# Weighing the values of a dilated attention: three split-precision products over the whole array, or plain fp32 with each head on its own half of the columns

## The chip, the cores and the metric

One core of a Trainium2 chip runs the whole program. The metric is the device time of one execution in microseconds (us). Engines are named as the profile names them: PE is TensorE (PEld its weight loads), DVE VectorE, ACT ScalarE, POOL GpSimd, SP SyncE.

## The reference, cut to what matters

One inference step of a two-layer decoder over a prompt of 1024 tokens and 8 sampled tokens. The change touches only the first mixer, and there the prompt. It projects the input to queries, keys and values for three dilation branches (window 128 and dilation 1, 512 and 4, 2048 and 16) and 16 heads of 64 features; each query reads at most 129 keys, which lie in its own block of 128 keys of its residue class and in the one before:

```python
s = jnp.einsum('nbqhd,nbphd->nhbqp', qb, kk).astype(jnp.float32) * SCALE
...
probs, lse = masked_softmax_lse(s, mask)
o = jnp.einsum('nhbqp,nbphd->nbqhd', probs, vv)     # the product that the change touches
...
y = merge_by_denominator(outs, lses).astype(x.dtype).reshape(B, S, N_HEADS_A * HEAD_DIM) @ w_o
```

After the mixer come a layer norm, a gated feed-forward part, a second mixer and a second feed-forward part. All inputs and outputs are fp32.

## The kernel before

**Split precision.** Most products are made of three: a value `a` is kept as `a_hi` (a cast to fp32r) and `a_lo` (the rest, `a - a_hi`, as fp32r), and `product` (lines 99 to 103) adds `w_hi*x_hi`, `w_hi*x_lo` and `w_lo*x_hi` in one bank. ACT writes the high parts, DVE or POOL the low ones. A few products take plain fp32 operands: those of the sampled tokens with their caches (`key_four`, line 1024; `value_four`, line 1062; a small one in the second mixer, line 2476). These, and their like for the sampled tokens of the second mixer, are the only ones that put several results on different columns of the array at a time, by `tile_position` or by the partitions that they write: four groups of 16 or 32 columns in the first two, two groups of 64 in the third.

**Order of the first mixer.** The work is cut into 24 items `i`, each a pair of heads `q` (8 pairs) and a dilation branch `g` (3). An item has 4 steps `s`, so there are 96 steps `u`; each attends two tiles of 128 queries (`j` = 0, 1), for both heads `h` of the pair. The order of each engine's queue is written out by hand in `body(u, i, s)`. On PE a step is: `scores(u)`, `weigh_values(u - 2)`, `transpose_probs(u - 1)`, in the first two steps of an item `transpose_v`, sometimes one or two small products that spread merge factors (`spread_factors`, line 911), and then two or three `chunk`s of the projection of the next item (line 101 to 103, 24 matmuls each of 352 or 328 columns). In the last four steps there is no next item, and `key_four` stands in the place of the chunks. After the steps come `value_four` and the merging of the last pair.

**The product of the change.** A query tile reads one or two key blocks `b`: two, except where its class has no block before it. That makes 35 blocks for each head pair over the three branches. For each block `weigh_values` runs one `product`: stationary operand `v_hi[:, kt, :]` or `v_lo`, 128 keys by 128 features (both heads side by side), moving operand 256 columns of turned probabilities `pt_hi` or `pt_lo` (128 queries of head 0, then 128 of head 1). The result is `pv_bank`, 128 feature rows by 2 x 2 x 128 columns, in which only the feature rows of head `h` with the query columns of head `h` are wanted. So half of the bank is never read. `evacuate_o` on ACT copies the wanted parts, 64 rows by 256 columns for each head.

**Around it.** ACT's `high_probs` and DVE's `low_probs` make `pt_hi` and `pt_lo` from the turned probabilities in `pt_bank`, `high_v` and `low_v` do it for the values in `x_bank`. In DVE's queue `low_probs(u - 1)` stands behind `mask_scores(u)` and ahead of `merge_tile`, whose product `a_fbm` (line 734) must be done before PE may run the next `spread_factors`.

Of the kernel before, what the change touches and what calls it, by code (L numbers as in the profile page):

```python
# [24 lines left out]
P = 128  # L25
# [30 lines left out]
def f32(ap):  # L56
    return ap.bitcast(F32)
# [105 lines left out]
def mixer_a(nc, x_hi, x_lo, dram, s_roll):  # L163
    ctx = ExitStack()
    sems = []
    with ctx:
# [9 lines left out]
        raw = sb("raw", [P, 2, KT, P])  # L176
        v_hi = sb("v_hi", [P, QT, P], F32R)
        v_lo = sb("v_lo", [P, QT, P], F32R)
        vt = sb("vt", [P, T])
# [8 lines left out]
        sp = sb("sp", [P, 2, 2, 2, 2 * P])  # L188
        pt_hi = sb("pt_hi", [P, 2, 4 * P], F32R)
        pt_lo = sb("pt_lo", [P, 2, 4 * P], F32R)  # L190
        o = sb("o", [P, 2, NG, T])
# [15 lines left out]
        with ExitStack() as lent:  # L207
# [20 lines left out]
        kq_out = [sem("kq_out0"), sem("kq_out1")]  # L228
        s_vout, s_vtr, s_vhi, s_vlo = (sem(x) for x in ("vout", "vtr", "vhi", "vlo"))
        s_scores, s_masked, s_probs, s_ptr, s_pthi, s_ptlo, s_pv, s_oev = (  # L230
            sem(x) for x in ("scores", "masked", "probs", "ptr", "pthi", "ptlo", "pv", "oev"))
        s_sttr, s_stcp, s_stout, s_srin, s_dve, s_dd, s_mw, s_f, s_fb, s_fbm, s_fbr, s_oout = (
# [210 lines left out]
        def _(act):  # L443
# [37 lines left out]
            def evacuate_o(u):  # L481


                i, s = divmod(u, SUPER)
                q, g = pair_group(i)
                need(act, s_pv, 2 * u + 2)
                if g == 0 and s == 0:
                    need(act, s_oout, 16 * (q - 1))
                for h in range(2):
                    rows = slice(HD * h, HD * h + HD)  # L490
                    src = pv_bank[rows, :].rearrange("p (i x q) -> p i x q", i=2, x=2)[:, :, h, :]
                    last = act.copy(pair_tokens(o[rows, q % 2, g, 0:SEQ], g, s), pair_shape(src, g))
                last.then_inc(s_oev, 1)

            def high_probs(u):
                need(act, s_pv, 2 * u)
                for j in range(2):
                    c0 = 2 * first_key(u, j)
                    need(act, s_ptr, 2 * u + j + 1)
                    act.copy(pt_hi[:, j, c0:], pt_bank[j][:, c0:]).then_inc(s_pthi, 1)  # L500

            def high_v(u, i, s):
                need(act, s_vtr, 2 * i + s + 1)
                need(act, s_pv, 2 * (u - 1))
                act.copy(v_hi[:, 4 * s:4 * s + 4, :].rearrange("p a b -> p (a b)"), x_bank[:, :]).then_inc(s_vhi, 1)

# [33 lines left out]
            def body(u, i, s):  # L540
                q, g = pair_group(i)
                if s in SPLIT_AT and 3 * (i + 1) + SPLIT_AT[s] < NB:
                    split_w(3 * (i + 1) + SPLIT_AT[s])
                if attends(u):
                    exponentials(u)
                if u == NU + 1:
                    copy_last_stats(0)
                if attends(u - 2):
                    evacuate_o(u - 2)
                if attends(u - 1):  # L550
                    high_probs(u - 1)
                if attends(u) and s < 2:
                    high_v(u, i, s)
# [100 lines left out]
        def _(dve):  # L654
# [99 lines left out]

            def low_probs(u):
                for j in range(2):
                    c0 = 2 * first_key(u, j)
                    need(dve, s_pthi, 2 * u + j + 1)
                    dve.tensor_tensor(pt_lo[:, j, c0:], pt_bank[j][:, c0:], f32(pt_hi[:, j, c0:]),
                                      ALU.subtract).then_inc(s_ptlo, 1)  # L760

            def low_v(i, s):
                need(dve, s_vhi, 2 * i + s + 1)
                dve.tensor_tensor(v_lo[:, 4 * s:4 * s + 4, :].rearrange("p a b -> p (a b)"), x_bank[:, :],
                                  f32(v_hi[:, 4 * s:4 * s + 4, :].rearrange("p a b -> p (a b)")),
                                  ALU.subtract).then_inc(s_vlo, 1)

            def turn(i1, r):
# [10 lines left out]
            def body(u, i, s):  # L779
# [17 lines left out]
                if attends(u) and s < 2:  # L797
                    low_v(i, s)
                if attends(u) and q > 0 and g == 1 and s < 2:
# [76 lines left out]
        def _(pe):  # L876
            def stats_transpose(q):
                need(pe, s_probs, 4 * NG * SUPER * q)
                need(pe, s_vlo, 2 * min(NG * q + 1, NI))
                need(pe, s_fbm, 8 * (q - 1))  # L880
                pe.transpose(x_bank[0:96, 0:P], st[:, (q - 1) % 2, :], ident[:, :]).then_inc(s_sttr, 1)

            def spread_stats(w):
# [5 lines left out]
                else:  # L889
                    pe.wait_ge(s_ptlo, 2 * NU)  # L890
                to = last_bank[w]
# [12 lines left out]
            def spread_factors(q, j):  # L904
# [3 lines left out]
                if j in (0, 4):  # L908
                    need(pe, s_vlo, 2 * min(NG * q + 2 + j // 4, NI))
                need(pe, s_fbm, 8 * (q - 1) + j)  # L910
# [20 lines left out]
            def weigh_values(u):  # L931
                i, s = divmod(u, SUPER)
                need(pe, s_oev, u)
                if s in (0, 2):
                    need(pe, s_vlo, 2 * i + 1 + s // 2)
                for j in range(2):
                    need(pe, s_ptlo, 2 * u + j + 1)
                    b0 = first_key(u, j) // P
                    for b in range(b0, 2):
                        kt = 2 * s + j - 1 + b  # L940
                        cols = slice(b * 2 * P, (b + 1) * 2 * P)
                        last = product(pe, pv_bank[:, 2 * P * j:2 * P * (j + 1)], v_hi[:, kt, :], v_lo[:, kt, :],
                                       pt_hi[:, j, cols], pt_lo[:, j, cols], b == b0, b == 1)
                    last.then_inc(s_pv, 1)

            def transpose_probs(u):
                for j in range(2):
                    need(pe, s_probs, 4 * u + 2 * j + 2)
                    need(pe, s_ptlo, 2 * (u - 1) + j + 1)
                    for b in range(first_key(u, j) // P, 2):  # L950
# [5 lines left out]
            def transpose_v(i, s):  # L956
                need(pe, s_evac, 9 * (i + 1))
                need(pe, s_vlo, 2 * i + s)
                q, g = pair_group(i)
# [85 lines left out]
            def value_four(n):  # L1045
# [9 lines left out]
                if n == NG:  # L1055
                    pe.wait_ge(s_ptlo, 2 * NU)
                    pe.wait_ge(s_lcp, 2)
# [1624 lines left out]
```

## Time and profile before

| what | value |
|---|---|
| median of 3 runs | 3226.95 us (3219.56 to 3236.51) |
| the profiled execution: from its first to its last instruction | 3217.9 us |
| first mixer, steps and end | up to about 1200 us of it |
| PE, PEld busy | 97%, 94% |
| DVE, ACT, POOL busy | 54%, 49%, 53% |

The profiled execution gives no time of its own beside its span; 3217.9 us is 1.7 us under the fastest of the three runs and 9.1 us under their median. In a row of a timeline a group of equal instructions is one row: its start, the time from its first start to its last end, and xN for their number. A matmul's own duration runs on into the next ones (they are pipelined), so what one costs is the distance from start to start. A plain fp32 matmul is two records, with two weight loads.

### The profile page before, as it was taken

How to read it: one execution, taken by the hardware profiler on the slowest of the kernel's cores; microseconds unless marked ns; L12 is line 12 of the kernel's file. 1: busy time of each engine (PE TensorE's matmuls, PEld its weight loads, DVE VectorE, ACT ScalarE, POOL GpSimd, SP SyncE). 2: the span in 40 equal slices, each digit the busy share in tenths (PEclk: the TensorE clock that was granted, in tenths of full speed). 3: DMA queues.
4: the chain of work that ended last, by engine and by line, in shares of the span. 5: the costliest groups of instructions: out<-in, count | busy, mean ns of one | idle time of the engine just before them, and what ended most of it. 6: DMA issues, size and time to landing. Idle time of an engine off the chain costs nothing. (4 is left out here: it accounts for less than half of the span.)

```text
span 3217.9 us, 55825 instructions
## 1 busy us (share of the span) xinstructions
PE 3111.2 (97%) x21245; PEld 3033.5 (94%) x21245; DVE 1729.2 (54%) x3649; ACT 1590.6 (49%) x3331; POOL 1701.3 (53%) x1421
## 2 busy tenths in 40 slices
PE   8999999999999979999999999999899999999997
PEld 7999999999999959999999999988799999999997
DVE  4445555454555546665363365389866653533653
ACT  4555555555555524454353354367745543533542
POOL 5555555555555604665465466454246654554653
PEclk9999999999999989999999999999999999999998
DMA  5766676677667385444444444321153444444442
GB/s 210 251 246 209 229 266 218 224 247 248 235 225 273 101 302 183 131 133 132 139 134 138 138 141 146 111 62 41 41 197 128 137 130 139 152 138 136 163 152 95
DMA packets 134218, 540.86 MB, mean 168 GB/s; under 512 B 24336, under 2 KB 48544, under 8 KB 131120
## 3 DMA queue, kind: packets, MB, share of 16 engines
q1 hardware_dynamic: 133440, 536.51, 49.3%
q8 instruction: 170, 2.79, 0.4%
q14 instruction: 96, 0.79, 0.1%
q0 software_dynamic: 224, 0.26, 0.1%
q10 hardware_dynamic: 288, 0.52, 0.0%
HBM read 497.55 MB, written 216.85 MB: 222 GB/s over the span
## 5 line engine op out<-in xcount | busy, mean ns | idle before, releaser
L1369 ACT CAST w_hi<-raw 128x1024 fp32r<-128x1024 f32 (+1 forms) x459 | 471.3, 1027 | 841.7 <-PE bank L103 795.6
L101 PE MATMUL bank<-x_hi,w_hi 128*128 128x352 f32 (+1 forms) x2208 | 711.9, 322 | 5.2 <-POOL w_lo L1487 3.9
L1568 DVE TENSOR_TENSOR w_lo<-raw,w_hi 128x1024 fp32r<-128x1024 f32 (+1 forms) x229 | 320.7, 1401 | 735.9 <-ACT w_hi L1369 735.8
L102 PE MATMUL bank<-x_lo,w_hi 128*128 128x352 f32 (+1 forms) x2208 | 705.9, 320 | 0.0
L103 PE MATMUL bank<-x_hi,w_lo 128*128 128x352 f32 (+1 forms) x2208 | 702.5, 318 | 0.0
L1487 POOL TENSOR_TENSOR w_lo<-raw,w_hi 128x1024 fp32r<-128x1024 f32 (+1 forms) x230 | 546.8, 2377 | 276.0 <-ACT w_hi L1369 276.0
L101 PE MATMUL a_gemm<-x_hi,a_w_hi 128*128 128x352 f32 (+1 forms) x1728 | 560.5, 324 | 11.1 <-DVE x_lo L659 11.1
L102 PE MATMUL a_gemm<-x_lo,a_w_hi 128*128 128x352 f32 (+1 forms) x1728 | 553.3, 320 | 0.0
L103 PE MATMUL a_gemm<-x_hi,a_w_lo 128*128 128x352 f32 (+1 forms) x1728 | 551.4, 319 | 0.0
L101 PE MATMUL bank<-t_h_hi,w_hi 128*128 128x352 f32 (+1 forms) x1440 | 465.0, 323 | 6.8 <-POOL t_h_lo L1507 5.6
L103 PE MATMUL bank<-t_h_hi,w_lo 128*128 128x352 f32 (+1 forms) x1440 | 461.9, 321 | 0.0
L102 PE MATMUL bank<-t_h_lo,w_hi 128*128 128x352 f32 (+1 forms) x1440 | 460.2, 320 | 0.0
L101 PEld LDWEIGHTS bank<-x_hi,w_hi 128*128 128x128 f32 x2208 | 414.8, 188 | 8.3 <-POOL w_lo L1487 5.0
L102 PEld LDWEIGHTS bank<-x_lo,w_hi 128*128 128x128 f32 x2208 | 415.3, 188 | 1.6
L103 PEld LDWEIGHTS bank<-x_hi,w_lo 128*128 128x128 f32 x2208 | 415.0, 188 | 0.0
L101 PEld LDWEIGHTS a_gemm<-x_hi,a_w_hi 128*128 128x128 f32 x1728 | 325.7, 188 | 13.5 <-issue 9.2
L102 PEld LDWEIGHTS a_gemm<-x_lo,a_w_hi 128*128 128x128 f32 x1728 | 326.0, 189 | 0.0
L103 PEld LDWEIGHTS a_gemm<-x_hi,a_w_lo 128*128 128x128 f32 x1728 | 325.3, 188 | 0.0
L1507 POOL TENSOR_TENSOR t_h_lo<-t_acc,t_h_hi 128x352 fp32r<-128x352 f32 (+1 forms) x132 | 129.0, 977 | 332.9 <-ACT t_h_hi L1391 332.9
L101 PEld LDWEIGHTS bank<-t_h_hi,w_hi 128*128 128x128 f32 x1440 | 273.5, 190 | 9.2 <-issue 7.8
L750 DVE CUSTOM_DVE_ANT_0 a_sp<-a_scores,a_mask 128x128 f32<-128x128 f32 (+1 forms) x384 | 112.1, 347 | 304.4 <-PE a_scores L103 303.8
L102 PEld LDWEIGHTS bank<-t_h_lo,w_hi 128*128 128x128 f32 x1440 | 272.9, 190 | 0.9 <-issue 0.5
(303 smaller groups left out, 5693.1 us busy)
## 6 DMA issues: line engine op xcount, KB each, us to landing
raw<-w_up SPq DMA_DIRECT2D x264, 512.0 KB, 3.6
roll<-cache SPq DMA_DIRECT2D x128, 1023.5 KB
raw<-w_down SPq DMA_DIRECT2D x96, 512.0 KB, 3.5
a_raw<-w_a SPq DMA_DIRECT2D x72, 512.0 KB, 3.6
roll<-cache SPq DMA_DIRECT2D x16, 2044.0 KB
raw<-w_o SPq DMA_DIRECT2D x48, 512.0 KB, 3.5
raw<-w_down SPq DMA_DIRECT2D x48, 384.0 KB, 3.2
vT<-a_vt SPq DMA_DIRECT2D x24, 516.0 KB, 5.9
```

What stands on the lines that cost most here:

```text
L101: pe.matmul(out, w_hi, x_hi, start=first, stop=False)
L102: pe.matmul(out, w_hi, x_lo, start=False, stop=False)
L103: return pe.matmul(out, w_lo, x_hi, start=False, stop=last)
L750: dve.tensor_tensor_reduce(out=sp[:, u % 2, j, h, w0:], in0=s_bank[h][:, 2 * P * j + w0:2 * P * (j + 1)], in1=mk, scale=1.0, scalar=3.0e38 ...
L1369: act.copy(w_hi[:, b % RING, cols], raw[:, b % RING, cols]).then_inc(s_whi, 1)
L1487: pool.tensor_tensor(w_lo[:, b % RING, cols], raw[:, b % RING, cols], f32(w_hi[:, b % RING, cols]), ALU.subtract).then_inc(s_wlo[0], 1)
L1507: pool.tensor_tensor(h_lo[:, m, 0:n], acc[:, unit(c, m) % 3, 0:n], f32(h_hi[:, m, 0:n]), ALU.subtract).then_inc(s_hlo, 1)
L1568: dve.tensor_tensor(w_lo[:, b % RING, cols], raw[:, b % RING, cols], f32(w_hi[:, b % RING, cols]), ALU.subtract).then_inc(s_wlo[1], 1)
```

## The change

The values `v` and the turned probabilities `pt` are kept as one fp32 tile each; `v_lo`, `pt_lo` and the two DVE functions that made them are gone, and ACT's cast becomes a copy of the same size. `weigh_values` runs, for each block and head, one plain fp32 matmul: stationary `v[:, kt, rows]`, 128 keys by the 64 features of that head, moving 128 columns of that head's probabilities, written to partitions `rows` of the bank by `tile_position=(0, 64*h)`. Only wanted results are made, and `evacuate_o` copies them in one instruction of 128 rows. What waited for DVE's semaphores (`s_ptlo`, `s_vlo`) waits for ACT's (`s_pt`, `s_vev`).

```diff
-            def high_probs(u):
+                src = pv_bank[:, 0:2 * P].rearrange("p (i q) -> p i q", i=2)
+                act.copy(pair_tokens(o[:, q % 2, g, 0:SEQ], g, s), pair_shape(src, g)).then_inc(s_oev, 1)
+
+            def turned_probs(u):
                 need(act, s_pv, 2 * u)
                 for j in range(2):
                     c0 = 2 * first_key(u, j)
                     need(act, s_ptr, 2 * u + j + 1)
-                    act.copy(pt_hi[:, j, c0:], pt_bank[j][:, c0:]).then_inc(s_pthi, 1)
+                    act.copy(pt[:, j, c0:], pt_bank[j][:, c0:]).then_inc(s_pt, 1)
...
-            def low_probs(u):
-                for j in range(2):
-                    c0 = 2 * first_key(u, j)
-                    need(dve, s_pthi, 2 * u + j + 1)
-                    dve.tensor_tensor(pt_lo[:, j, c0:], pt_bank[j][:, c0:], f32(pt_hi[:, j, c0:]),
-                                      ALU.subtract).then_inc(s_ptlo, 1)
...
-                if attends(u - 1):
-                    low_probs(u - 1)
...
                 for j in range(2):
-                    need(pe, s_ptlo, 2 * u + j + 1)
+                    need(pe, s_pt, 2 * u + j + 1)
                     b0 = first_key(u, j) // P
                     for b in range(b0, 2):
                         kt = 2 * s + j - 1 + b
-                        cols = slice(b * 2 * P, (b + 1) * 2 * P)
-                        last = product(pe, pv_bank[:, 2 * P * j:2 * P * (j + 1)], v_hi[:, kt, :], v_lo[:, kt, :],
-                                       pt_hi[:, j, cols], pt_lo[:, j, cols], b == b0, b == 1)
+                        for h in range(2):
+                            c, rows = (2 * b + h) * P, slice(HD * h, HD * h + HD)
+                            last = pe.matmul(pv_bank[rows, P * j:P * (j + 1)], v[:, kt, rows], pt[:, j, c:c + P],
+                                             start=(b == b0), stop=(b == 1), tile_position=(0, HD * h))
                     last.then_inc(s_pv, 1)
```

PE's queue in a step of the third branch with two blocks and no `transpose_v` (`a_scores` is the scores bank, `a_pv` the product of the change, `a_probsT` the turning of the probabilities, `a_gemm` the projection), before:

```order
L102 MATMUL a_scores<-a_kq_lo,a_kq_hi 128x128
L103 MATMUL a_scores<-a_kq_hi,a_kq_lo 128x128
L101 MATMUL a_pv<-a_pt_hi,a_v_hi 128x256
L102 MATMUL a_pv<-a_pt_lo,a_v_hi 128x256
L103 MATMUL a_pv<-a_pt_hi,a_v_lo 128x256
L101 MATMUL a_pv<-a_pt_hi,a_v_hi 128x256
L102 MATMUL a_pv<-a_pt_lo,a_v_hi 128x256
L103 MATMUL a_pv<-a_pt_hi,a_v_lo 128x256
L953 MATMUL a_probsT<-a_ident,a_sp 128x128 x4
L101 MATMUL a_gemm<-x_hi,a_w_hi 128x328
```

and now:

```order
L102 MATMUL a_scores<-a_kq_lo,a_kq_hi 128x128
L103 MATMUL a_scores<-a_kq_hi,a_kq_lo 128x128
L921 MATMUL a_pv<-a_pt,a_v 64x128 x4
L932 MATMUL a_probsT<-a_ident,a_sp 128x128 x4
L101 MATMUL a_gemm<-x_hi,a_w_hi 128x328
```

The place in the queue is the same; six matmuls of 256 columns have become four of 128 columns, which are eight records, since they are plain fp32.

DVE's queue in the last but one step of the last item (u = 94; `a_sp,a_st` are the masked scores, `a_fbm` and `a_o` the two halves of `merge_tile`), before:

```order
L750 ISA a_st 128x1
L759 TENSOR_TENSOR a_pt_lo<-a_probsT,a_pt_hi 128x256 x2
L734 TENSOR_TENSOR a_fbm<-a_vT_factors,a_o 128x384
L737 TENSOR_REDUCE a_o<-a_fbm 128x128
L734 TENSOR_TENSOR a_fbm<-a_vT_factors,a_o 128x384
L737 TENSOR_REDUCE a_o<-a_fbm 128x128
L750 ISA a_sp,a_st<-a_scores,a_mask 128x128
```

and now:

```order
L745 ISA a_st 128x1
L729 TENSOR_TENSOR a_fbm<-a_vT_factors,a_o 128x384
L732 TENSOR_REDUCE a_o<-a_fbm 128x128
L729 TENSOR_TENSOR a_fbm<-a_vT_factors,a_o 128x384
L732 TENSOR_REDUCE a_o<-a_fbm 128x128
L745 ISA a_sp,a_st<-a_scores,a_mask 128x128
```

The two `a_pt_lo` instructions, which waited for ACT, no longer stand between the masking and the merge.

## Rows read from the trace of the kernel before

**Rows 1.** The page, its head and busy times.

```profile
span 3217.9 us, 55825 instructions
...
PE 3111.2 (97%) x21245; PEld 3033.5 (94%) x21245; DVE 1729.2 (54%) x3649; ACT 1590.6 (49%) x3331; POOL 1701.3 (53%) x1421
```

**Rows 2.** Windows: stretch, its length, busy us (instructions) by engine, PEclk, DMA share, GB/s.

```profile
100.00:1110.00 1010.00, 1008.25 (x7258) 979.07 (x7256) 520.93 (x1522) 573.57 (x1556) 553.06 (x459) 1.00 0.65 227
...
1200.00:3217.90 2017.90, 1950.63 (x12642) 1924.86 (x12642) 1123.28 (x1914) 943.77 (x1591) 1077.88 (x889) 0.99 0.40 130
```

**Rows 3.** Waits of PE, 100 to 1110 us: total us, times, longest.

```profile
PE a_vT_factors L911 <- DVE a_fbm L734: 1.8, 2, 1.6
```

**Rows 4.** All instructions that touch a_pv (two lines): duration ns min/median/max.

```profile
L101 PE MATMUL a_pv<-a_pt_hi,a_v_hi x280: 277/280/580, 76.1 to 1156.2; 128*128 128x256 f32 x140
...
L492 ACT COPY a_o<-a_pv x192: 345/590/642, 79.2 to 1157.4; 64x256 f32<-64x256 f32 x192
```

**Rows 5.** Timeline of PE, one step: start us, us.

```profile
607.12 0.29 PE L103 MATMUL a_scores<-a_kq_hi,a_kq_lo 64*128 64x256 f32 x2
607.34 0.39 PE L101 MATMUL a_pv<-a_pt_hi,a_v_hi 128*128 128x256 f32 x1
607.56 0.28 PE L102 MATMUL a_pv<-a_pt_lo,a_v_hi 128*128 128x256 f32 x1
...
608.03 0.28 PE L103 MATMUL a_pv<-a_pt_hi,a_v_lo 128*128 128x256 f32 x1
608.15 0.60 PE L953 MATMUL a_probsT<-a_ident,a_sp 128*128 128x128 f32 x4
```

**Rows 6.** Timeline of PE, first and last rounds of one key_four (plain fp32, four column groups).

```profile
1120.58 0.28 PE L1024 MATMUL a_gemm<-a_raw,a_cos 128*16 128x128 f32 x1
1120.58 0.30 PE L1024 MATMUL a_gemm<-a_units_kv,a_cos 128*16 128x128 f32 x3
...
1120.70 0.29 PE L1024 MATMUL a_gemm<-a_units_kv,a_cos 128*16 128x128 f32 x3
...
1122.23 0.29 PE L1024 MATMUL a_gemm<-a_units_kv,a_cos 128*16 128x128 f32 x3
```

**Rows 7.** Timeline of PEld at the same place: the loads of the third round.

```profile
1120.70 0.11 PEld L1024 LDWEIGHTS a_gemm<-a_units_kv,a_cos 128*16 128x16 f32 x3
```

**Rows 8.** Timeline, then the source line: plain fp32 on two 64-column halves, in the second mixer.

```profile
2327.18 0.31 PEld L2476 LDWEIGHTS bank<-b_d_own_x,b_d_om 128*64 128x64 f32 x8
2327.18 0.43 PE L2476 MATMUL bank<-b_d_own_x,b_d_om 128*64 128x32 f32 x8
...
L2476 PEld LDWEIGHTS bank<-b_d_own_x,b_d_om x8: 133/137/138, 2327.2 to 2327.4; 128*64 128x64 f32 x8
```

**Rows 9.** Groups of ACT and DVE, 100 to 1110 us: busy us, mean ns, idle before.

```profile
L538 ACT COPY a_vt<-a_gemm 128x352 f32<-128x352 f32 x43 | 19.5, 453 | 9.5 <-PE a_gemm L103 9.4
...
L759 DVE TENSOR_TENSOR a_pt_lo<-a_probsT,a_pt_hi 128x512 fp32r<-128x512 f32 x81 | 53.9, 688 | 38.1 <-ACT a_pt_hi L500 35.7
```

**Rows 10.** Waits of PE, 1110 to 1200 us, two of them.

```profile
PE a_vT_factors L911 <- DVE a_fbm L734: 6.0, 6, 1.8
...
PE a_scores L1062 <- DMA a_units_kv<-cache: 3.2, 1, 3.2
```

**Rows 11.** Timeline of DVE, then of PE, in step u = 94.

```profile
1136.67 0.08 DVE L750 DVE_READ_ACCUMULATOR2_ANT a_st<- 128x1 f32 x1
1139.31 0.76 DVE L759 TENSOR_TENSOR a_pt_lo<-a_probsT,a_pt_hi 128x256 fp32r<-128x256 f32 x2 [2.56 <-ACT a_pt_hi L500]
1139.98 0.55 DVE L734 TENSOR_TENSOR a_fbm<-a_vT_factors,a_o 128x384 f32<-128x384 f32 x1
...
1140.58 0.44 PE L911 MATMUL a_vT_factors<-a_f_both,a_sel 128*128 128x384 f32 x1 [1.47 <-DVE a_fbm L734]
```

**Rows 12.** Windows of ten us in the mixer's end; columns as in rows 2.

```profile
1140.00:1150.00 10.00, 6.27 (x107) 5.49 (x107) 7.01 (x21) 5.02 (x16) 0.00 (x0) 1.00 0.81 304
1150.00:1160.00 10.00, 9.10 (x176) 7.88 (x176) 3.96 (x13) 3.25 (x8) 0.00 (x0) 0.83 1.02 407
```

More of the change, by code:

```diff
@@ L176, in mixer_a @@
         raw = sb("raw", [P, 2, KT, P])
-        v_hi = sb("v_hi", [P, QT, P], F32R)
-        v_lo = sb("v_lo", [P, QT, P], F32R)
+        v = sb("v", [P, QT, P])
         vt = sb("vt", [P, T])
@@ L188, in mixer_a @@
         sp = sb("sp", [P, 2, 2, 2, 2 * P])
-        pt_hi = sb("pt_hi", [P, 2, 4 * P], F32R)
-        pt_lo = sb("pt_lo", [P, 2, 4 * P], F32R)
+        pt = sb("pt", [P, 2, 4 * P])
         o = sb("o", [P, 2, NG, T])
@@ L228, in mixer_a @@
         kq_out = [sem("kq_out0"), sem("kq_out1")]
-        s_vout, s_vtr, s_vhi, s_vlo = (sem(x) for x in ("vout", "vtr", "vhi", "vlo"))
-        s_scores, s_masked, s_probs, s_ptr, s_pthi, s_ptlo, s_pv, s_oev = (
-            sem(x) for x in ("scores", "masked", "probs", "ptr", "pthi", "ptlo", "pv", "oev"))
+        s_vout, s_vtr, s_vev = (sem(x) for x in ("vout", "vtr", "vev"))
+        s_scores, s_masked, s_probs, s_ptr, s_pt, s_pv, s_oev = (
+            sem(x) for x in ("scores", "masked", "probs", "ptr", "pt", "pv", "oev"))
         s_sttr, s_stcp, s_stout, s_srin, s_dve, s_dd, s_mw, s_f, s_fb, s_fbm, s_fbr, s_oout = (
@@ L488, in evacuate_o @@
                     need(act, s_oout, 16 * (q - 1))
[L489 to L493, printed above, removed]
-            def high_probs(u):
+                src = pv_bank[:, 0:2 * P].rearrange("p (i q) -> p i q", i=2)
+                act.copy(pair_tokens(o[:, q % 2, g, 0:SEQ], g, s), pair_shape(src, g)).then_inc(s_oev, 1)
+            def turned_probs(u):
                 need(act, s_pv, 2 * u)
@@ L499, in high_probs, with evacuate_v @@
                     need(act, s_ptr, 2 * u + j + 1)
-                    act.copy(pt_hi[:, j, c0:], pt_bank[j][:, c0:]).then_inc(s_pthi, 1)
-            def high_v(u, i, s):
+                    act.copy(pt[:, j, c0:], pt_bank[j][:, c0:]).then_inc(s_pt, 1)
+            def evacuate_v(u, i, s):
                 need(act, s_vtr, 2 * i + s + 1)
                 need(act, s_pv, 2 * (u - 1))
-                act.copy(v_hi[:, 4 * s:4 * s + 4, :].rearrange("p a b -> p (a b)"), x_bank[:, :]).then_inc(s_vhi, 1)
+                act.copy(v[:, 4 * s:4 * s + 4, :].rearrange("p a b -> p (a b)"), x_bank[:, :]).then_inc(s_vev, 1)
             def high_turned(i1, r):
@@ L550, in body @@
                 if attends(u - 1):
-                    high_probs(u - 1)
+                    turned_probs(u - 1)
                 if attends(u) and s < 2:
-                    high_v(u, i, s)
+                    evacuate_v(u, i, s)
                 if stats_due(i, s):
@@ L753, in mask_scores @@
                                                  accum_out=st[:, q % 2, c:c + 1]).then_inc(s_masked, 1)
-            def low_probs(u):
-                for j in range(2):
-                    c0 = 2 * first_key(u, j)
-                    need(dve, s_pthi, 2 * u + j + 1)
-                    dve.tensor_tensor(pt_lo[:, j, c0:], pt_bank[j][:, c0:], f32(pt_hi[:, j, c0:]),
-                                      ALU.subtract).then_inc(s_ptlo, 1)
[L762 to L766, printed above, removed]
             def turn(i1, r):
@@ L792, in body @@
                     replicate_stats(0)
-                if attends(u - 1):
-                    low_probs(u - 1)
                 if u == NU:
                     replicate_stats(1)
-                if attends(u) and s < 2:
-                    low_v(i, s)
                 if attends(u) and q > 0 and g == 1 and s < 2:
@@ L878, in stats_transpose @@
                 need(pe, s_probs, 4 * NG * SUPER * q)
-                need(pe, s_vlo, 2 * min(NG * q + 1, NI))
+                need(pe, s_vev, 2 * min(NG * q + 1, NI))
                 need(pe, s_fbm, 8 * (q - 1))
@@ L889, in spread_stats @@
                 else:
-                    pe.wait_ge(s_ptlo, 2 * NU)
+                    pe.wait_ge(s_pt, 2 * NU)
                 to = last_bank[w]
@@ L908, in spread_factors @@
                 if j in (0, 4):
-                    need(pe, s_vlo, 2 * min(NG * q + 2 + j // 4, NI))
+                    need(pe, s_vev, 2 * min(NG * q + 2 + j // 4, NI))
                 need(pe, s_fbm, 8 * (q - 1) + j)
@@ L934, in weigh_values @@
                 if s in (0, 2):
-                    need(pe, s_vlo, 2 * i + 1 + s // 2)
+                    need(pe, s_vev, 2 * i + 1 + s // 2)
                 for j in range(2):
-                    need(pe, s_ptlo, 2 * u + j + 1)
+                    need(pe, s_pt, 2 * u + j + 1)
                     b0 = first_key(u, j) // P
@@ L948, in transpose_probs @@
                     need(pe, s_probs, 4 * u + 2 * j + 2)
-                    need(pe, s_ptlo, 2 * (u - 1) + j + 1)
+                    need(pe, s_pt, 2 * (u - 1) + j + 1)
                     for b in range(first_key(u, j) // P, 2):
@@ L957, in transpose_v @@
                 need(pe, s_evac, 9 * (i + 1))
-                need(pe, s_vlo, 2 * i + s)
+                need(pe, s_vev, 2 * i + s)
                 q, g = pair_group(i)
@@ L1055, in value_four @@
                 if n == NG:
-                    pe.wait_ge(s_ptlo, 2 * NU)
+                    pe.wait_ge(s_pt, 2 * NU)
                     pe.wait_ge(s_lcp, 2)
```

## The prediction

> **What bounds the kernel now.** I read the page first, for who is busy: PE 97% of a span of 3217.9 us, the others about half [rows 1]. A share is an average over stages, so windows come next: from 100 to 1110 us, where the first mixer's steps run, PE is busy for 1008.25 of 1010 us, while DVE, ACT and POOL have 521 to 574 us of work [rows 2]. Busy is not yet bound, since matmuls overlap, so the third view is PE's waits in that stretch: 1.8 us in all [rows 3]. There PE's queue alone sets the pace, at full clock (1.00, that is 2.4 GHz), and what it is spared there shortens the program. From 1200 us on nothing is changed. From 1110 to 1200 us, the mixer's end, PE does wait: 6.0 us for DVE's merge, 3.2 us in one piece for a transfer [rows 10]; there the sum must be made otherwise.
>
> So the question is what the product of the change costs on PE, from start to start, with what stands before and behind it. A timeline of one step shows it [rows 5]. Between neighbours of the old product the distance is 0.118 us (607.56 to 608.03 is four distances, 0.47). From the last scores matmul (607.12) to the second of the product (607.56) there are 0.44 us where two steps at pace would be 0.24: changing from the scores' form (64 rows of the array, two at once) to the full array costs 0.20 us. It comes in two equal parts: the array runs empty (607.34 is 0.22 behind 607.12, 0.10 more than pace), and then the first weight load has nothing to hide behind (0.22 to the next start, 0.10 more than pace). From the product to the turning of the probabilities (608.03 to 608.15) there is no such cost; both use the full array.
>
> **The change on PE.** There are 280 blocks [rows 4] in 96 steps (192 copies by ACT, two a step [rows 4]).
> - Removed: three matmuls a block, 3 x 0.118 = 0.354 us.
> - Added: two plain fp32 matmuls a block, each two records. What a record of 128 moving columns costs is shown by the sampled tokens' keys, plain fp32 too: rounds start at 1120.58 and 1122.23, first and last of 16, so 1.65 / 15 = 0.110 us a round [rows 6], and a round is four records on four column groups (one and three in the rows). So a record takes 0.110 us of its own group, and groups run beside each other. For two halves a block then takes two rounds: 0.220 us. Saved: 0.134 x 280 = 37.5 us.
> - Are 64-column weight loads hidden? Each record has one. In the second mixer eight of them, on two halves, take 0.31 us in all and 0.137 each [rows 8]: (0.31 - 0.137) / 3 = 0.058 us from pair to pair if they go in pairs, and one behind the other they would be 0.025 apart, which is less than half of what a full 128-column load shows (0.10, above). So they go in pairs, 0.058 us each, and that fits under a pass of 0.110. That loads run under a pass on the same group is seen in the keys: the loads of the third round start at 1120.70, with the second round of matmuls and not behind it [rows 6, 7]. The record of 64 columns with 128 moving ones is in no row; it lies between the keys (16 columns) and the full array (128 columns, whose loads of 0.10 are hidden under 0.118), and I take it as hidden.
> - Moved: the forms now change twice in a step. Scores to halves: 0.20 as before, less what the shorter first load saves, 0.10 - 0.06, so 0.16. Halves to the turning: 0.20, new. Net 0.16 + 0.20 - 0.20 = 0.16, by the finer starts 0.15; x 96 = 14.4 us. I could price this last change of form from 0.10 (emptying alone) to 0.20; the load behind it is a full one, so I take the upper end.
> - Sum for PE: 37.5 - 14.4 = 23.1 us saved.
>
> **The change on ACT and DVE.** ACT makes one copy of 128 rows instead of two of 64 rows, 0.590 us each [rows 4]; rows side by side cost nothing (128x352 takes 453 ns [rows 9]), so it saves some 0.5 us a step. DVE loses `low_probs` (688 ns each for the wide ones [rows 9]) and `low_v`. In the plateau this is worth nothing in itself, for PE does not wait. It does remove the 1.8 us of [rows 3]: PE waits there for a merge that stands behind `low_probs` in DVE's queue. I take 1 us. In the mixer's end the same pattern is plain: in step 94 DVE is done with the masks at 1136.67 + 0.08, waits 2.56 us for ACT's cast, makes `a_pt_lo`, and only then the merge at 1139.98, for which PE waits 1.47 us [rows 11]. With `low_probs` gone nothing of that chain is left; about 3.3 of the 6.0 us lie in steps 94 and 95. But behind it the DMA engines are full, 1.02 of their time from 1150 us against 0.81 just before [rows 12], and the caches that they bring are asked for by PE's progress: PE's gain starts the transfers earlier, and the full stretch keeps its length. I take 2 us of 3.3, and 0.7 us off the steps' own gain, since five of the 96 lie here among waits. Bounds: from -1 (nothing comes through) to 4.
>
> Sum: 23.1 + 1 + 2 - 0.7 = 25.4 us. On the profiled span 3217.9 that gives 3192.5; on the median 3226.95, which is what is compared, 3201. What the cover is: nothing of this is hidden, PE's work counts one to one as long as its waits in the plateau stay near 1.8 us.
>
> **A rule against the change.** The rows of the keys have four groups whose matmuls use all 128 rows of the array, and loads and matmuls of different groups and of the same group run at one time [rows 6, 7]. The Trainium skill says otherwise ("TensorE: Matmul & The Clock Gate", Part 3, what overlaps and what doesn't): a weight load runs beside matmuls in flight only when its row group is another one. By that rule nothing of a block would overlap here; the trace does not agree. The same page measures three column groups at 2.38 times one; the rows here show four rounds' worth in each 0.110 us, four times one. By its factor (0.79 of ideal), an estimate from that page, a block would take 0.28 us and the sum for PE would be 6 us instead of 23.
>
> **Rivals.**
> 1. The halves do not run together: 4 x 0.110 = 0.44 us a block, 0.086 more than before, x 280 = +24, and +14.4 for the forms: +38, less the 3 us elsewhere: 3262 us. This is the one on the other side. It decides from 0.303 us a block (0.354 - 14.4/280): from there on the change of form costs more than the passes save. For it: no row has two halves with long moving operands. Against: [rows 6], and the pairs of [rows 8].
> 2. The halves run together, but a 64-column load is not hidden under its pass: 2 x (0.110 + 0.058) = 0.336 us a block, -5 and +14.4 us, less 3: 3233 us. Against: hidden loads in [rows 5] and [rows 7].
> 3. Everything in a row, each load before its pass and one half after the other: 4 x 0.168 = 0.67 us a block, +89 and +14, less 3: 3327 us. Against: [rows 6] and [rows 7]. It is the first rule of the Trainium skill above.
> 4. Part or all of the gain goes elsewhere: in the plateau another engine becomes the bound once PE is 2% faster, or the end of the mixer waits for transfers as long as before: 3217 to 3227 us. Against: POOL, the nearest chain, has 553 of 1010 us of work, and DMA 0.65 [rows 2].
> 5. The halves disturb each other in part: a block midway between the forecast and rival 2, 0.28 us, saves 20.7 and costs 14.4, with 3 elsewhere: 3218 us. Against: four groups do not disturb each other in [rows 6]. The second figure of the Trainium skill above comes out there.
>
> **How the numbers follow.** My forecast 0.78, with a range of its own from 3191 to 3212 (end of the mixer -1 to 4, change of form 0.10 to 0.20 a step dearer or cheaper by 5 us, and the spread of the three runs, 0.26% to either side); rival 1 0.07, rival 2 0.06, rival 3 0.02, rival 4 0.04, rival 5 0.03. The range for 8 in 10 goes from 3188 to 3226, which takes in rival 5 and most of rival 4. A measurement of this kernel tells about 0.5% (16 us) from no change: faster is the forecast without its upper edge, 0.74; same is that edge and rivals 2, 4 and 5, 0.17; slower is rivals 1 and 3, 0.09.
>
> **What would show it.** In the changed profile's timeline of a step: eight or more 64-column records in pairs 0.110 us apart, 0.22 us a block; 0.16 us lost ahead of them and 0.20 behind, where before there was 0.00; PE's step shorter by 0.40 us with four blocks and 0.12 with two; no wait of PE for `a_fbm` in steps 94 and 95; the mixer's end near 1175 us instead of 1200, and from there on the same length. I am wrong if a block takes 0.33 or 0.44 us, or if waits of PE appear in the plateau.

## The result, and the profile after

The changed kernel takes 3198.98 us (median of 4 runs, 3194.4 to 3200.22), the kernel before 3228.39 us on the same chip (median of 4, 3219.56 to 3236.51): a ratio of 0.9913, 95% interval 0.9892 to 0.9934. Forecast were 3201 us and a ratio of 0.992. So the total is within 2 us. Its terms were not all right: misses of some 5 us with opposite signs cancel in it, as the sections below show.

The page of the changed kernel, its head and busy times:

```profile
span 3198.6 us, 56049 instructions
...
PE 3088.3 (97%) x21525; PEld 2991.3 (94%) x21525; DVE 1619.6 (51%) x3409; ACT 1526.4 (48%) x3235; POOL 1700.5 (53%) x1421
```

PE's share is 97% as in [rows 1]; busy shares say nothing of the gain. DVE lost 110 us of work. The windows of the steps and of all that follows the first mixer (columns as in [rows 2]):

```profile
100.00:1110.00 1010.00, 1002.20 (x7784) 956.03 (x7782) 424.53 (x1329) 524.16 (x1502) 564.40 (x484) 1.00 0.67 233
1175.00:3198.60 2023.60, 1953.45 (x12642) 1927.34 (x12642) 1126.55 (x1914) 944.53 (x1591) 1080.01 (x889) 0.98 0.41 130
```

The second stretch holds the same 12642 matmuls as the second row of [rows 2], and begins 25 us earlier. PE's timeline in a step with three blocks shows the product of the change (start, time to the last end, xN):

```profile
1084.10 0.29 PE L103 MATMUL a_scores<-a_kq_hi,a_kq_lo 64*128 64x256 f32 x2
1084.32 0.88 PE L921 MATMUL a_pv<-a_pt,a_v 128*64 128x128 f32 x12
1085.12 0.87 PE L932 MATMUL a_probsT<-a_ident,a_sp 128*128 128x128 f32 x6
1085.75 0.42 PE L889 MATMUL a_vT_factors<-a_f_both,a_sel 128*128 128x384 f32 x1
```

Twelve records of 64 columns and the turning behind them: 0.80 us from the first record of the one to the first of the other. At 0.110 us a pair, six pairs are 0.66 us; the other 0.14 is the price of changed forms. By the starts of the single records 0.04 of it lie within the product (the second pair comes 0.153 us behind the first) and 0.10 behind its last pair. A last 0.055 lies behind the first matmul of the turning, and 0.10 ahead of the product, as before. Over the whole first mixer, from the last scores matmul to the second matmul of the turning, a step took 1.130, 1.485 or 1.851 us before (medians; two, three or four blocks; 32, 40 and 24 steps) and takes 0.957, 1.178 or 1.396 now. That is 32 x 0.173 + 40 x 0.307 + 24 x 0.455 = 28.7 us on the steps alone; 23.1 were forecast.

PE's waits, 100 to 1080 us and then in the mixer's end (1085 to 1176 us): total us, times, longest.

```profile
PE a_vT_factors L889 <- DVE a_fbm L729: 3.6, 1, 3.6
PE a_scores L101 <- POOL a_kq_lo L600: 0.4, 1, 0.4
...
PE a_scores L1041 <- DMA a_units_kv<-cache: 5.5, 2, 4.7
PE a_gemm L1003 <- DMA a_units_kv<-k_dec: 4.1, 2, 3.6
PE bank L1709 <- PEq L84: 3.9, 1, 3.9
PE a_gemm L1010 <- DMA a_rot<-spread: 3.8, 1, 3.8
PE a_vT_factors L889 <- DVE a_fbm L729: 2.7, 4, 0.7
```

The first row is new: one wait of 3.6 us in a stretch where the longest was 1.6 [rows 3]. In the mixer's end the waits for the merge fell from six with 6.0 us to four with 2.7, and those for the caches rose from 3.2 to 5.5 [rows 10].

The same matmuls of both kernels can be laid side by side, since all but the product's are the same and in the same order. The times that follow are those of the kernel before. The changed kernel is ahead of it, in its profiled run, by 4.4 us at 249 us, by 1.1 at 327, by 23.4 at 1106, by 28.8 at 1154, by 24.3 at 1194 and by 19.3 at the end; at 74 us, ahead of the first step, it was 0.4 behind. So about 5 us of the steps' gain are lost between 249 and 327 us, and 4.5 between 1154 and 1194. Of these, some 2 us are the longer wait for the caches. Some 2 more go in matmuls that ran at half clock (1.2 GHz) in the changed kernel and mostly at full clock in the kernel before. Windows of nearly the same matmuls, before and after (PEclk 0.83 and 0.50):

```profile
1184.00:1194.00 10.00, 6.68 (x36) 1.77 (x36) 5.89 (x10) 0.00 (x0) 0.00 (x0) 0.83 0.56 222
1158.00:1168.00 10.00, 8.74 (x35) 2.05 (x35) 4.61 (x8) 0.00 (x0) 0.00 (x0) 0.50 0.46 182
```

The last 5 us go behind the mixer, where nothing was changed, in pieces: windows in which PE was granted half clock fell otherwise. A second profiled run of the kernel before was 7.5 us longer than the first (3225.4 against 3217.9), 5 of them ahead of 1217 us; the first lies near that kernel's fastest run, and its half-clock windows in the mixer's end sum to 27 us against 41 in the second. Against the second profile the changed kernel is 29.7 us ahead at 1194 us and 26.8 at the end. So most of the gap between the 19 us of the profiles and the 29 of the medians is that the first profile of the kernel before was of a fast run.

### The profile page after: what moved, and what is told of

It is laid out like the page before. It is cut to its first block and busy times, and to the rows that moved or that the text cites. A ratio compares the mean times of both kernels' runs of the same rounds, so it can differ in the third digit from the quotient of the medians.

```text
span 3198.6 us, 56049 instructions
## 1 busy us (share of the span) xinstructions
PE 3088.3 (97%) x21525; PEld 2991.3 (94%) x21525; DVE 1619.6 (51%) x3409; ACT 1526.4 (48%) x3235; POOL 1700.5 (53%) x1421
```

## Experiments

Each ran on one chip with runs of the kernel before among its own. The kernel before had a median of 3224.65 us (13 runs) beside experiments 1 to 4, 3227.59 (12) beside 5 to 8 and 3226.26 (15) beside 9 to 11.

**1. Both heads on the same half.** Columns 0 to 63 for head 0 and head 1, one behind the other; the results go to different columns of the bank, and ACT copies them in two.

```diff
-   pe.matmul(pv_bank[rows, P * j:P * (j + 1)], v[:, kt, rows], pt[:, j, c:c + P], ..., tile_position=(0, HD * h))
+   pe.matmul(pv_bank[0:HD, P * (2 * j + h):P * (2 * j + h + 1)], v[:, kt, rows], pt[:, j, c:c + P], ..., tile_position=(0, 0))
```

> The changed kernel, but both heads' products run on columns 0 to 63, one head's blocks after the other's, into different columns of the bank, and ACT evacuates with two copies of 64 rows. Same 64-column plain fp32 instructions, same number, no running beside each other. My theory (each record takes 0.110 us of its own half, and what the change wins is that the halves run at once): a block takes 0.44 us instead of 0.22, 280 blocks, so 62 us slower than the changed kernel, 33 us slower than before (ratio to before 1.010). Rival (the halves never ran at once, or something else hid the products): same time as the changed kernel, ratio 0.991.

Measured: 3250.47 us (3248.52 to 3251.3), ratio 1.0081, 1.0066 to 1.0096. PE's timeline of a step with two blocks:

```profile
610.44 0.28 PE L103 MATMUL a_scores<-a_kq_hi,a_kq_lo 64*128 64x128 f32 x2
...
610.65 1.09 PE L923 MATMUL a_pv<-a_pt,a_v 128*64 128x128 f32 x8
611.67 0.66 PE L934 MATMUL a_probsT<-a_ident,a_sp 128*128 128x128 f32 x4
```

Eight records of two blocks take 1.02 us to the turning; in the changed kernel twelve of three blocks take 0.80. Rival 1 is what the kernel would do if the halves did not run together, and it is slower than before, as its bound (0.303 us a block) said. It did not reach the 3262 us given for it: at 1106 us this kernel is 50.7 us behind the changed one, where 0.22 x 280 = 62 was expected for the whole. By then 89 of the 96 products have run (58 of the 62 us), and the changed kernel has lost 5.4 us to a wait near 265 us that this slower one does not have (below): 53, and 2 us stay open.

**2. Plain fp32, but on the full array.** One matmul a block, 128 columns, 256 moving; no halves, so no change of form between product and turning.

```diff
-   for h in range(2):
-       ... pe.matmul(pv_bank[rows, ...], v[:, kt, rows], pt[:, j, c:c + P], ..., tile_position=(0, HD * h))
+   last = pe.matmul(pv_bank[:, 2 * P * j:2 * P * (j + 1)], v[:, kt, :], pt[:, j, cols], start=(b == b0), stop=(b == 1))
```

> The changed kernel, but one plain fp32 matmul a block on the full array: stationary 128 x 128 (both heads), moving 256 columns, bank and evacuation as before. No change of form behind the scores but the one that was there. My theory: two records a block, each 256 columns at 0.86 ns each (0.110 us for 128), so 0.44 us a block, +0.08 x 280 = +23 us to before, less 2 to 4 us that ACT and DVE give at the mixer's end: ratio 1.006. Rival (plain fp32 operands themselves are what wins): ratio under 1.

Measured: 3242.44 us (3240.64 to 3244.09), ratio 1.0057, 1.004 to 1.0074. PE's timeline, the product and what follows:

```profile
608.01 1.13 PE L922 MATMUL a_pv<-a_pt,a_v 128*128 128x256 f32 x4
608.97 0.38 PE L933 MATMUL a_probsT<-a_ident,a_sp 128*128 128x128 f32 x2
```

Four records of 256 columns for two blocks, 0.96 us: 0.10 for the first load and 0.215 each. A block is 0.43 us where three fp32r products were 0.354. So giving up the split precision is a loss by itself (0.08 us a block); the gain is the halves'.

**3. The order of the halves.** The loop over the heads outside that over the key blocks: two blocks of head 0, then two of head 1.

```diff
-   for b in range(b0, 2):
-       for h in range(2):
+   for h in range(2):
+       for b in range(b0, 2):
```

> The changed kernel with the loops over block and head exchanged: all records of head 0 (four where there are two blocks), then all of head 1. Theory A (each half has a queue of its own deep enough, as the keys show, where four groups start together though their records stand two by two): no change, ratio 0.991. Theory B (the engine starts in program order and looks ahead only a little): in tiles with two blocks the second head starts late by one to three records of 0.11 us, and nothing overlaps behind; 184 of 192 pairs of products at most, 88 of them with two blocks: 88 x 0.11 to 0.33 = 10 to 29 us slower than the changed kernel, ratio 0.994 to 1.000.

Measured: 3200.03 us (3198.57 to 3201.46), ratio 0.9925, 0.991 to 0.994, and 21.8 us ahead at 1106 us against 23.4. In a step of two blocks each query tile has one, so there the program's order is the same in both kernels; the test is in the 64 steps of three and four blocks. PE's timeline, a step of four, of this kernel and then of the changed one:

```profile
507.15 1.15 PE L921 MATMUL a_pv<-a_pt,a_v 128*64 128x128 f32 x16
508.23 0.98 PE L932 MATMUL a_probsT<-a_ident,a_sp 128*128 128x128 f32 x7
```

```profile
506.84 1.09 PE L921 MATMUL a_pv<-a_pt,a_v 128*64 128x128 f32 x16
507.87 0.98 PE L932 MATMUL a_probsT<-a_ident,a_sp 128*128 128x128 f32 x7
```

Sixteen records take 1.075 us to the turning, against 1.025 in the changed kernel and 1.89 in experiment 1 (single records). So the halves run beside each other even when two blocks of the one stand ahead of two of the other. It costs 0.05 us in each step of three or four blocks and nothing in those of two: 3 us in all, far from Theory B's 10 to 29, but not Theory A's nothing. The medians, whose intervals overlap, cannot tell 3 us.

**4. Two more changes of form a step.** The product of `j` = 0 ahead of the turning, that of `j` = 1 behind it.

```diff
-   weigh_values(u - 2)
-   transpose_probs(u - 1)
+   weigh_values(u - 2, 0)
+   transpose_probs(u - 1)
+   weigh_values(u - 2, 1)
```

> The changed kernel, but PE weighs the first query tile of a step ahead of the turning of the probabilities and the second behind it, so that each step has one more time on the halves: two more changes of form. My theory: a change from the full array to the halves costs 0.10 of emptying and 0.06 of first load, the one back 0.10 and 0.06 (the profile after shows 0.165 to the second turning matmul, not 0.21): 0.31 x 96 = 29 us slower than the changed kernel, back to the time of before, ratio 1.000. Rival (a change of form costs nothing once the queue runs ahead): ratio 0.991.

Measured: 3227.28 us (3223.79 to 3232.54), ratio 1.0007, 0.9997 to 1.0017. All of the gain is gone, with not one matmul more. PE's timeline:

```profile
599.77 0.28 PE L103 MATMUL a_scores<-a_kq_hi,a_kq_lo 64*128 64x128 f32 x2
599.98 0.44 PE L921 MATMUL a_pv<-a_pt,a_v 128*64 128x128 f32 x4
600.35 0.66 PE L932 MATMUL a_probsT<-a_ident,a_sp 128*128 128x128 f32 x4
600.94 0.44 PE L921 MATMUL a_pv<-a_pt,a_v 128*64 128x128 f32 x4
601.30 0.44 PE L889 MATMUL a_vT_factors<-a_f_both,a_sel 128*128 128x384 f32 x1
```

599.98 to 600.35 is 0.37 us for a block of 0.22: 0.15 for changed forms. The added run costs 0.14 the same way. Behind it come L889 and the projection: from the product's last record to the projection's first there are 0.48 us, where in the changed kernel there are 0.29 from the last of the turning (single records). I put the 0.20 more down to emptying, 0.10, and the load of a split product in the open, 0.10. That is 0.14 + 0.20 = 0.34 a step; in the 44 steps in which values are turned behind the added run (a load of 140 ns, see below) it is 0.30. At 1106 us the kernel is 26.2 us behind the changed one. Of this, 2.6 us arose ahead of the first step, where the kernels are the same; with the 5.4 us that the wait near 265 us costs the changed one it makes 29.0, or 0.33 a step over the 89 products run by then. The Trainium skill ("TensorEngine Tiling (Array Packing)", Key Properties) says that switching the tiling mode drains the array. The rows agree: 0.14 to 0.16 us a change to or from the halves, 0.20 where a split product comes next.

**5. Without the low parts.** The kernel before, with PE's three products all of the high parts (so the weighed values are three times the high product) and DVE's `low_probs` and `low_v` left out: what the change does on DVE, alone.

```diff
-   last = product(pe, pv_bank[...], v_hi[:, kt, :], v_lo[:, kt, :], pt_hi[:, j, cols], pt_lo[:, j, cols], b == b0, b == 1)
+   last = product(pe, pv_bank[...], v_hi[:, kt, :], v_hi[:, kt, :], pt_hi[:, j, cols], pt_hi[:, j, cols], b == b0, b == 1)
```

> The kernel before, with the low parts of the values and probabilities left out: DVE does not make them, and PE runs the same three matmuls a block with the high parts in their place. So it has the relief of DVE and the shorter wait for the operands, and none of PE's part. My theory: nothing in the plateau; PE's waits for the merge in the last item's steps (6.0 us in all before) mostly go, and the transfers behind take back a part of it: 1 to 4 us faster, ratio 0.999, same within noise. Rival (a large part of the change's gain is DVE's relief): 10 us or more, ratio under 0.997.

Measured: 3218.59 us (3215.3 to 3222.08), ratio 0.9973, 0.9963 to 0.9983: 8.7 us, more than the 1 to 4 expected, and the interval reaches into the rival's (a ratio under 0.997). Its profile shows only part of it: 2.7 us ahead of the second profile of the kernel before at 1106 us (5.0 at the end), 0.6 ahead of the first (2.5 behind it at the end). Experiments 1 and 2 have the same relief of DVE. Their steps alone, read as above, cost 31.8 and 21.1 us more than before, and they were 26.1 and 18.4 us slower: 5.7 and 2.7 us for the relief, each within some 5 us. So it is not clear how much of the change's 28 us is the relief; no stretch shows more than these few us, and the rest stays open.

**6. Two steps' products in one run.** `weigh_values` every second step for two steps, with two buffers each for `pt` and `v` and the two halves of the bank; half as many changes of form, nothing else.

```diff
-   if attends(u - 2):
-       weigh_values(u - 2)
+   if u % 2:
+       for w in (u - 3, u - 2):
+           if attends(w):
+               weigh_values(w)
```

> The changed kernel, but PE weighs the values of two steps together, every second step (values and turned probabilities get two buffers, which take the room of the low parts; each of the two steps has its own half of the bank, and both are evacuated when both are done). In 48 of 96 steps the three forms (scores, halves, full) become two. My theory: a step without the product saves the emptying and the first load of one change, 0.16 us, 48 x 0.16 = 7 us faster than the changed kernel, ratio to before 0.989. Rival (the longer evacuation and burst make PE wait): not faster than the changed kernel, with waits of PE for a_o or a_pt in the profile.

Measured: 3190.79 us (3187.98 to 3191.66), ratio 0.9884, 0.9871 to 0.9898, 6.2 us less than the changed kernel in runs on the same chip (3197.0 us, experiment 7). PE's timeline, sixteen records in one run:

```profile
607.04 1.09 PE L924 MATMUL a_pv<-a_pt,a_v 128*64 128x128 f32 x16
608.07 0.55 PE L935 MATMUL a_probsT<-a_ident,a_sp 128*128 128x128 f32 x3
```

It is 7.8 us ahead of the changed kernel at 1106 us, for some 45 steps that have no product: 0.17 us each. Such a step goes from scores to turning for 0.15 us (single records) where it had two changes for 0.29, so 0.14 were to be had.

**7 and 8. The two kernels again.** Is the wait near 265 us chance?

> The changed kernel as it is, timed again for a narrower interval beside the runs of this call, and a second profile. In the one profile at hand the gain is 23 us at the end of the plateau, with one wait of PE of 3.6 us near 265 us and half clock for 3.4 us behind it. My theory: that wait is chance of the transfers and not of the change; by the steps' own times the gain is 28 us: ratio 0.991. Rival (the wait belongs to the change): it stands in the second profile too.

> The kernel before, profiled a second time, to see what of the wait for the merge near 545 us and of the windows at half clock stays from run to run. If chance: the steps' own times are the same to 0.01 us, and waits and half-clock windows stand elsewhere.

Measured: 3197.0 us (3195.78 to 3200.55), ratio 0.9904, 0.9889 to 0.9919, with the wait there again:

```profile
PE a_vT_factors L889 <- DVE a_fbm L729: 3.5, 1, 3.5
PE a_scores L101 <- POOL a_kq_lo L600: 1.2, 2, 0.9
```

The kernel before (one run, 3227.0 us) again has none at that place. Between 245 and 300 us the wait is 2.9 us in experiment 3 and 3.2 in 6, 0.9 in 4 and 5, and there is none in 1 and 2, the slowest. So the theory of chance fell, and the wait goes mainly with the pace. Not with the pace alone: at 249 us experiment 4 is 2.9 us behind the kernel before and experiment 5 is 0.4 behind, and yet they wait where it does not. The chain behind the wait was looked up in the changed kernel, on POOL, DVE and PE:

```profile
265.60 0.93 POOL L589 TENSOR_TENSOR a_qp<-a_ev,a_cos 128x352 f32<-128x352 f32 x1 [5.84 <-DMA kT<-a_qp]
...
267.71 0.01 DVE L757 LOAD_MASK_SELECT a_rot<-a_ev  x1 [8.85 <-POOL a_qp L593]
...
269.37 0.44 PE L889 MATMUL a_vT_factors<-a_f_both,a_sel 128*128 128x384 f32 x1 [3.64 <-DVE a_fbm L729]
...
270.00:275.00 5.00, 5.00 (x38) 4.49 (x37) 4.85 (x15) 3.18 (x8) 3.76 (x4) 0.66 0.01 2
```

POOL waits 5.84 us until the store of turned keys has landed and freed a buffer; DVE, one turn further, waits 8.85 for POOL, and `merge_tile` stands behind that in its queue; PE waits for the merge, and then runs a window at half clock (PEclk 0.66 on average in the window row). In the kernel before, the store lands at nearly the same time, but POOL comes to wait for it 5 us later (264.7 against 259.8):

```profile
266.20 0.95 POOL L594 TENSOR_TENSOR a_qp<-a_ev,a_cos 128x352 f32<-128x352 f32 x1 [1.51 <-DMA kT<-a_qp]
```

In experiment 5 POOL gets on only at 268.4 us, 2.2 us later than here, at the same pace: when the store lands varies too, and counts. What would set that time is the DMA engines. The windows from 225 to 265 us, of the changed kernel and of the kernel before:

```profile
225.00:265.00 40.00, 40.00 (x308) 38.47 (x307) 18.41 (x52) 18.25 (x52) 16.13 (x13) 1.00 1.00 356
```

```profile
225.00:265.00 40.00, 40.00 (x293) 38.98 (x292) 22.80 (x69) 21.21 (x62) 19.45 (x15) 1.00 0.95 335
```

They are full in both. In that stretch SP copies caches ("roll"), two pieces a step, and four of them are large:

```profile
roll<-cache SPq DMA_DIRECT2D x4, 2044.0 KB
```

**9 to 11. The cache copies evened out.** Of each quarter of the caches the four 2.0 MB pieces went two in a step; now each goes with one of 64 KB. Pieces, bytes and the steps that issue them stay. Made with the changed kernel, with the kernel before, and with the kernel of experiment 6.

```diff
-            pieces = [piece for it in range(4) for piece in roll_pieces(dram, it)]
+            pieces = []
+            for it in range(4):
+                p = roll_pieces(dram, it)
+                pieces += p[0:32] + [piece for a, b in zip(p[32:36], p[40:44]) for piece in (a, b)] + p[36:40]
```

> The changed kernel, with the copies of the caches in another order: of each quarter the four 2.0 MB pieces no longer go two in a step (4.1 MB in each of two steps) but each with one of the 64 KB pieces; the number of pieces, the bytes and the steps that issue them stay. Theory A: the 3.6 us for which PE waits near 265 us in the changed kernel come from these two heavy steps. DMA engines are full there (share about 1.0 from 225 to 265 us in both kernels), the store of turned keys lands at nearly the same time in both (265.6 and 266.2 us) though it is asked for 4 us earlier, GpSimd waits for it, VectorE's turn behind that, then the merge, then PE; half clock follows. Then the wait goes with the heavy steps, and the time falls by 3.6 us of wait and 2 to 4 us of half clock behind it: near 3192, ratio to the changed kernel about 0.998, to the kernel before 0.989. Theory B: the store is late for another reason (its place in the queue, its form): the wait stays at 3 us or more and the time is that of the changed kernel.

> The same new order of the cache copies in the kernel before, as a control. Theory A: PE does not wait near 265 us there (GpSimd waits 1.5 us for the store, which slack takes up), so the time is unchanged within 2 us, apart from the 1.6 us wait near 550 us, which may go. If it became faster by 5 us or more, the order would be a gain by itself and no part of the account of this change.

> Both together: the products of two steps in one run (as in the kernel that beat both), and the cache copies evened out. Theory A: its PE wait of 3.2 us near 268 us goes as well, 4 to 6 us less than the 3190.8 of the former: 3185 to 3187. Theory B: 3190 to 3191.

Measured:

| kernel | us | ratio to before |
|---|---|---|
| changed, copies evened | 3188.82 (3184.36 to 3190.36) | 0.9881, 0.9867 to 0.9894 |
| before, copies evened | 3222.28 (3218.52 to 3228.4) | 0.9988, 0.9979 to 0.9997 |
| experiment 6, copies evened | 3185.67 (3182.33 to 3186.88) | 0.9875, 0.986 to 0.989 |

With the copies evened the changed kernel and that of experiment 6 show no wait of PE from 100 to 1080 us. Of the changed kernel with even copies, the instruction of POOL that waited 5.84 us for the store, and the windows:

```profile
258.33 0.94 POOL L592 TENSOR_TENSOR a_qp<-a_ev,a_cos 128x352 f32<-128x352 f32 x1
...
225.00:265.00 40.00, 40.00 (x313) 38.23 (x313) 21.07 (x58) 19.14 (x54) 20.40 (x17) 1.00 0.80 279
```

Between the matmuls at 249 and at 327 us it gains 2.1 us on the kernel before, where the changed kernel lost 3.3: the wait cost 5.4 us, 3.6 of waiting and half of one 3.4 us window at half clock. At 1106 us it is 30.8 us ahead; 1.4 us of its lead over the changed kernel arose ahead of the first step. The control gained 1.3 us there, by the wait of 1.6 us near 550 us that goes with the second quarter's large pieces, and about 4 by the medians, just beyond what was expected of it and just short of the 5 that would have made the new order a gain by itself. So Theory A holds for the wait: it goes with the heavy steps. Of the time, 3188.82 us are 8 to 10 less than the changed kernel's 3197.0 and 3198.98, and 3 less than expected; some 4 of them the control has too. What is left, 4 to 6 us, fits the 5.4, but the intervals are not narrow enough to show it by themselves. For experiment 6 the profiles say 5.9 us at 1106 us, but the ratios (0.9884 and 0.9875) have overlapping intervals; there the gain of evening is less sure.

## Why the prediction was right, and where it was not

**The mechanism and the passes.** Halves in pairs 0.110 us apart, 0.22 us a block, 37.5 us for 280 blocks: as forecast from [rows 6]. Experiments 1 and 3 show that the two halves of the columns make it, and 2 that plain fp32 without them is a loss. Rivals 1, 2, 3 and 5 fell with the timeline of a step.

**The change of form: right in kind, too dear in size.** The step that failed: "the load behind it is a full one, so I take the upper end". What the text calls emptying costs 0.10 us, as priced. The exposed load behind it costs 0.055, not 0.10, from the halves to the turning. The reason could be read beforehand: a weight load's own row. PEld's timeline, product, turning and the next product:

```profile
1084.32 0.63 PEld L921 LDWEIGHTS a_pv<-a_pt,a_v 128*64 128x64 f32 x12
1085.12 0.64 PEld L932 LDWEIGHTS a_probsT<-a_ident,a_sp 128*128 128x128 f32 x6 [0.17 <-issue]
1085.72 0.19 PEld L889 LDWEIGHTS a_vT_factors<-a_f_both,a_sel 128*128 128x128 f32 x1
```

and the loads of the turning by themselves, 100 to 1110 us, now and in the kernel before (min/median/max ns):

```profile
L932 PEld LDWEIGHTS a_probsT<-a_ident,a_sp x519: 137/140/230, 112.7 to 1110.0; 128*128 128x128 f32 x173
L953 PEld LDWEIGHTS a_probsT<-a_ident,a_sp x508: 137/141/146, 114.0 to 1109.3; 128*128 128x128 f32 x170
```

A load of the turning, 128 columns, takes 140 ns as the product's 64-column loads do, not 190 as a product of split parts. So the two changes cost 0.29 us together (0.14 and 0.15) where 0.16 and 0.20 were taken: 0.06 to 0.07 a step, some 6 us over 96 steps. It is the difference between the 23.1 us forecast and the 28.7 measured.

**The plateau: the one us gained was 5.4 us lost.** The step that failed: "nothing of this is hidden, PE's work counts one to one as long as its waits in the plateau stay near 1.8 us", and with it rival 4's "against", a DMA share of 0.65 over 1010 us [rows 2]. The mean hid a stretch of 40 us with a share of 0.95, next to which a chain over POOL and DVE had 1.5 us of wait already. PE arrived 4 to 5 us earlier there and met transfers that ended when they had before. Experiment 7 shows that the wait belongs to the change, and 9 to 11 that it goes with the large copies. It is rival 4 in small, and it was not among the terms. (By [rows 2] ACT, with 574 us, had more work than the POOL that rival 4 calls nearest; the chain that bound ran over POOL's wait, not over its work.)

**The mixer's end.** The waits for the merge in steps 94 and 95 went, as said: all of their 3.3 us, not 2. The four others, of the last pair, stayed. With the own gain of the last seven products, 1.6 us (the prediction counted five), the kernel gained 5.4 us between 1106 and 1154 us. Behind it 4.5 us were lost again. The windows 1120 to 1160 us, of the changed kernel:

```profile
1120.00:1160.00 40.00, 27.92 (x286) 15.37 (x290) 19.12 (x52) 4.58 (x14) 0.00 (x0) 0.85 1.02 404
```

The full stretch began earlier and stayed full, as the text said, and the waits for the caches grew by some 2 us. The other 2 us, of matmuls at half clock behind it, were no term of the sum; whether the change brings them is not shown, since the half-clock windows there fell otherwise in each profile. The mixer ended at 1175.63 us, 24.3 ahead (1175 forecast).

**The sum.** On the profiled runs: steps 28.7, the waits of [rows 3] 1.8, the wait at 265 us -5.4, mixer's end and the start about -0.8; 24.3 at 1194 us, where 25.4 were forecast for the whole. It is right to 1 us by luck, by errors that cancel: +5.6 for the forms, -4.6 in the plateau (-3.6 for +1), -2.1 in the mixer's end (-0.8 for 2 - 0.7). The medians moved by 29.4 and, in the second comparison, 30.6 us, some 5 more. Against the second profile of the kernel before the gain at 1194 us is 29.7, so these 5 us are within what one kernel's runs differ by. The leaving out of the low parts, which by itself gave 8.7 us (experiment 5) where three were taken, may have a part in it; no profile shows the place.

## What to carry to other kernels

Two heads of 64 features that are multiplied with both heads' weights waste half of the array. With its own columns for each, a block of plain fp32 took 0.22 us here instead of 0.43. That pays only if the forms change seldom: count the changes (here 0.14 to 0.20 us each) before the passes, and put runs of one form together. Read each exposed load (one with no pass to hide behind) from its own row, not from that of another operation. And before PE is made faster, look for short stretches with full DMA engines and a small wait on a helper's chain, not at the mean: what was gained ahead of such a place can be lost there (here 5.4 us).

## What was not expected of the hardware

- The halves hardly depend on each other's order: with two blocks of head 0 ahead of two of head 1 in the program, sixteen records took 1.075 us to the turning (experiment 3), 0.05 more than block by block, where all on one half they took 1.89 (experiment 1).
- A weight load of 128 rows by 128 columns takes 140 ns for the turning and 190 for the split products, and exposes 0.055 us against 0.10.
- Behind the wait near 265 us (3.6, 3.5, 2.9, 3.2 us) PE was granted half clock for 3.4 us in the changed kernel, in its repetition and in experiments 3 and 6; with the copies evened there is neither. The kernel before waited near 550 us for 1.6 us in its first profile, with no half clock behind it, and for 1.9 in its second, with 3.4 us of it. So a wait can cost more than its length.
